# The last stage of a decoder block's kernel joined to its trunk's program part

## What is computed

```python
h = rmsnorm(x, g_pre) * (1 + scale) + shift
p = h @ w_in                                   # 1024 -> 8704, cut into branches
# four token mixers: pooling, gated recurrence, short convolution, differential attention
gates = sigmoid(m_g)                           # 4 x 1024 columns of p
merged = (gates[0] * (y_pool @ w_merge_pool) + gates[1] * (y_hgrn @ w_merge_hgrn)
        + gates[2] * (y_conv @ w_merge_conv) + gates[3] * (y_diff @ w_merge_diff))
out = merged @ w_out
x = x + gate * rmsnorm(out, g_post)
```

## Time and profile before

| | us |
|---|---|
| median of 3 runs | 2377.98 (2377.79 to 2378.16) |
| profiled execution | 2383.72 |
| its span, first to last instruction | 2381.9 |
| TensorE busy in it | 2238.5 |
| VectorE, ScalarE, GpSimd busy | 1500.5, 1137.0, 849.5 |
| mean granted clock of TensorE | 0.973 |

### The profile page before, as it was taken

One profiled execution on the slowest core, in us unless ns is written; L12 is line 12 of the kernel. 1 busy time (PEld: TensorE's weight loads), 2 busy tenths in 40 slices (PEclk: granted clock), 3 DMA queues, 4 the chain that ended last, 5 costly groups with the idle time before them and its releaser, 6 DMA issues. The chain is left out here.

```text
span 2381.9 us, 35169 instructions
## 1 busy us (share of the span) xinstructions
PE 2238.5 (94%) x11573; PEld 1858.6 (78%) x11573; DVE 1500.5 (63%) x2681; ACT 1137.0 (48%) x2416; POOL 849.5 (36%) x747
## 2 busy tenths in 40 slices
PE   4798999999999999899999999999999978899998
PEld 4587788877777778787888888878888856787886
DVE  6766777748888795445777666445556436375571
ACT  4653566635454444444666666333434234444351
POOL 1222333426565563021232222133434206254452
PEclk7899999999999999999999999999999989999999
DMA  7778888678777778947566565588878766465561
GB/s 268 275 232 305 271 261 265 230 256 291 267 248 263 254 241 277 338 140 236 169 183 182 156 194 157 166 277 244 251 239 255 220 255 236 158 222 194 185 225 62
DMA packets 336940, 544.82 MB, mean 229 GB/s; under 512 B 26592, under 2 KB 216448, under 8 KB 331904
## 3 DMA queue, kind: packets, MB, share of 16 engines
q1 hardware_dynamic: 306528, 432.56, 54.4%
q10 hardware_dynamic: 30240, 110.11, 14.8%
HBM read 326.04 MB, written 221.77 MB: 230 GB/s over the span
## 5 line engine op out<-in xcount | busy, mean ns | idle before, releaser
L1791 PE MATMUL gb<-h_hi,w_both 128*128 128x512 f32 x1904 | 782.5, 411 | 54.2 <-ACT o L1013 25.5
L1793 PE MATMUL gb<-h_hi,w_both 128*128 128x512 f32 x1904 | 753.4, 396 | 0.0
L1792 PE MATMUL gb<-h_lo,w_both 128*128 128x512 f32 x1904 | 751.4, 395 | 0.0
L1791 PEld LDWEIGHTS gb<-h_hi,w_both 128*128 128x128 f32 x1904 | 363.7, 191 | 136.1 <-issue 64.4
L1793 PEld LDWEIGHTS gb<-h_hi,w_both 128*128 128x128 f32 x1904 | 362.6, 190 | 80.1
L1792 PEld LDWEIGHTS gb<-h_lo,w_both 128*128 128x128 f32 x1904 | 364.7, 192 | 66.8 <-issue 0.2
L1013 ACT ACTIVATE o<-gb 128x512 f32<-128x512 f32 x272 | 161.6, 594 | 343.1 <-PE gb L1793 297.6
L1078 ACT ACTIVATE C_prob<-C_sc,C_negm 128x512 f32<-128x512 f32 (+3 forms) x320 | 198.4, 622 | 223.4 <-DVE C_negm L1411 214.5
L881 POOL TENSOR_TENSOR C_prob<-C_prob,C_cf 128x512 f32<-128x512 f32 (+3 forms) x160 | 160.6, 1028 | 367.9 <-DVE C_cf L1433 363.3
L1323 DVE TENSOR_TENSOR o<-gb,o 128x512 f32<-128x512 f32 x204 | 140.1, 687 | 200.8 <-PE gb L1793 191.5
L1313 DVE TENSOR_TENSOR w_both<-w,w_both 128x512 fp32r<-128x512 f32 x190 | 164.9, 868 | 128.7 <-ACT w_both L990 128.3
(11 more groups left out here) (236 smaller groups left out, 3757.9 us busy)
## 6 DMA issues: line engine op xcount, KB each, us to landing
wS_scratch<-w_both SPq DMA_DIRECT2D x210, 512.0 KB, 3.7
w_both<-wS_scratch ACTq DMA_DIRECT2D x210, 512.0 KB, 4.6
w<-in_w_in_dram SPq DMA_DIRECT2D x76, 512.0 KB, 5.2
gT_scratch<-o SPq DMA_DIRECT2D x128, 256.0 KB, 4.9
D_gate<-gT_scratch SPq DMA_DIRECT2D x32, 1024.0 KB, 5.0
pT_scratch<-o SPq DMA_DIRECT2D x80, 256.0 KB, 4.4
D_wm_stage<-wm_scratch SPq DMA_DIRECT2D x32, 640.0 KB, 6.1
C_qt<-qB_scratch SPq DMA_DIRECT2D x128, 128.0 KB, 3.6
```

The costliest lines, as they stand in the source:

```text
L1791: mm(to, hi[:, k, :], h_hi[j][:, k, :], start=(fresh and k == 0), stop=False, skip_group_check=True)
L1792: mm(to, hi[:, k, :], h_lo[j][:, k, :], start=False, stop=False, skip_group_check=True)
L1793: last = mm(to, lo[:, k, :], h_hi[j][:, k, :], start=False, stop=(k == KH - 1), skip_group_check=True)
```

## The change

The last stage is now a class `LastStage`, whose parts for each engine are called at the end of the trunk's lists. The second block, with the leaving of the first, is gone. Its semaphores are those of the trunk's beginning, used again. Its text in the loops is the same but for these points:

- **Loads beside the last products.** SP issues y of the first group in slot 468 (behind `mixers_over(1)`), merge weights 0 in slot 470, gates 0 and 1 in 472 and 473, merge weights 1 in 475, each when the product whose buffers it overwrites is done. The buffers of the last stage are laid over the trunk's operands so that this is early.
- **Splits beside the last products.** Two chunks of y in each of the slots 472 to 476, weights 0 in slot 475, on ScalarE and VectorE; the first sigmoid in slot 485 of ScalarE's list.
- **Mixers.** The last eight blocks are 11 or 12 slots apart, the last at slot 452.
- **Buffers.** `wo_stage` is gone: `wo_in` has three buffers (o_buf0, o_buf1, x_in), which with post first hold y. SP issues w_out's first three slices, post, gates 2 and weights 2 only in its own part, behind the landing of all trunk outputs. The result of the squares, which nobody reads, goes into gate buffer 2 in place of wo_stage.
- **Store.** The store of a group's last block stands in step 0 ahead of the loads, in place of step 1.
- GpSimd begins when the last product is done and all outputs have landed.

```diff
-MIX_BASE = [130 + 12 * i for i in range(8)] + [372 + 25 * i // 2 for i in range(8)]
+MIX_BASE = [130 + 12 * i for i in range(8)] + [372 + 23 * i // 2 for i in range(8)]
+LAST = MIX_BASE[-1] + 16
+LAST_UNIT = PRODUCTS - PER
...
-        wo_in = (wo_stage, o_buf[0], o_buf[1], x_in)
+        wo_in = (o_buf[0], o_buf[1], x_in)
+        y_first = [y[:, :] for y in y_stage] + [t[:, TG * z:TG * z + TG] for t in (o_buf[0], o_buf[1], x_in, post) for z in range(2)]
+        junk = gate[2][:, 0:2, :].rearrange("p b t -> p (b t)")
...
                 for d in range(KD):
                     n = KD * g + d
+                    if d == 0 and not first:
+                        store(TB * g - 1, TB - 1, row_before)
                     if not (last and d + 2 >= KD):
                         load_gates(n + 2, (d + 2) % KD, at if d + 2 < KD else at_next)
                         load_wm(n + 2, (d + 2) % KD)
                     if first and d + NW < KD:
                         load_wo(d + NW)
-                    if d == 1 and not first:
-                        store(TB * g - 1, TB - 1, row_before)
...
+                if n == LAST:
+                    mixers_over(1)
+                    last_stage.first_y(sp)
+                if n == LAST_UNIT + 1:
+                    sp.wait_ge(packed, 16 * 4 * KD)
+                    sp.wait_ge(product_done, LAST_UNIT + 1)
+                    last_stage.first_wm(sp, 0)
+                for d in range(2):
+                    if n == LAST_UNIT + 3 + d:
+                        sp.wait_ge(product_done, LAST_UNIT + 2 + d)
+                        last_stage.first_gates(sp, d)
+                if n == LAST_UNIT + 6:
+                    sp.wait_ge(product_done, LAST_UNIT + 4)
+                    last_stage.first_wm(sp, 1)
...
-            mixers_over(1)
-            sp.wait_ge(packed, 16 * 4 * KD)
-            sp.sem_clear(packed)
             for b in range(4):
                 sp.wait_ge(o_stored[b], COUNTS.o_total[UNITS - 1][b])
+            last_stage.on_sync(sp)
...
+                if 0 <= n - LAST - 4 < YC // 2:
+                    for k in range(2):
+                        last_stage.y_high(act, 0, 2 * (n - LAST - 4) + k)
+                if n == LAST_UNIT + 6:
+                    act.wait_ge(product_done, LAST_UNIT + 2)
+                    last_stage.wm_high(act, 0, 0, 0)
+                if n == SLOTS - 1:
+                    last_stage.gate_sigmoids(act, 0, 0, 0)
...
+                if 0 <= n - LAST - 4 < YC // 2:
+                    for k in range(2):
+                        last_stage.y_low(dve, 0, 2 * (n - LAST - 4) + k)
+                if n == LAST_UNIT + 6:
+                    last_stage.wm_low(dve, 0, 0)
```

More of the change, by code:

```diff
@@ L180, in banks @@
             return lambda name, shape: stack.enter_context(nc.psum_tensor(tag + name, shape, F32))
+        mem = Memory()
+        with ExitStack() as low_part:
+            sb = tensors(low_part, "D_")
+            wm = [[sb(f"wm{j}_{name}", [P, YC, P], dt) for name, dt in (("stage", F32), ("hi", F32R), ("lo", F32R))] for j in range(1)]
+            sb("pad0", [P, 2 * P])
+            mem.gate = [sb(f"gate{j}", [P, 4, TG]) for j in range(2)]
+            wm += [[sb(f"wm{j}_{name}", [P, YC, P], dt) for name, dt in (("stage", F32), ("hi", F32R), ("lo", F32R))] for j in range(1, 2)]
+            sb("pad1", [P, 2 * P])
+            mem.wo_lo = [sb(f"wo_lo{j}", [P, D], F32R) for j in range(4)]
+            mem.gate += [sb(f"gate{j}", [P, 4, TG]) for j in range(2, 4)]
+            mem.m_hi, mem.m_lo = sb("m_hi", [P, KD, TG], F32R), sb("m_lo", [P, KD, TG], F32R)
+            mem.wo_hi = sb("wo_hi", [P, KD, D], F32R)
+            wo_lo_last = [sb(f"wo_lo{j}", [P, D], F32R) for j in range(5, 8)]
+            mem.wm_stage, mem.wm_hi, mem.wm_lo = ([w[y] for w in wm] for y in range(3))
+        with ExitStack() as pair:
+            mem.pb = [None, pair.enter_context(nc.psum_tensor("D_pb1", [P, D], F32))]
         sb = tensors(ctx, "")
@@ L292, in trunk @@
             b6, b7 = ps("b6", [P, 4, P]), ps("b7", [P, 4, P])
+        with ExitStack() as fourth:
+            sb, ps = tensors(fourth, "D_"), banks(fourth, "D_")
+            mem.y_stage = [sb(f"y_stage{j}", [P, TG]) for j in range(2)]
+            mem.o_buf = [sb(f"o_buf{j}", [P, D]) for j in range(2)]
+            mem.x_in, mem.post = sb("x_in", [P, D]), sb("post", [P, D])
+            mem.y_hi, mem.y_lo = sb("y_hi", [P, YC, TG], F32R), sb("y_lo", [P, YC, TG], F32R)
+            mem.wo_lo += [sb("wo_lo4", [P, D], F32R)] + wo_lo_last
+            mem.ss, mem.rstd = sb("ss", [P, 1]), sb("rstd", [P, 1])
+            mem.mb = [ps(f"mb{b}", [P, TG]) for b in range(4)]
+            mem.pb[0] = ps("pb0", [P, D])
         w1_loaded, w2_loaded = sem("w1_loaded"), [sem(f"w2_loaded{j}") for j in range(2)]
@@ L371, in lo_count @@
             return h_lo_ready, hi_count(half, j, kk)
-        packed = x_in[0]
+        packed = start[0]
+        late = iter(start[1:])
+        last_stage = LastStage(nc, mem, lambda: next(late), x, wmP, w_out, gT, yT, post_d, out, epsb)
         block = ctx.enter_context(nc.Block())
@@ L965, in _ @@
                     decays_second(i)
+            pool.wait_ge(product_done, PRODUCTS)
+            for b in range(4):
+                pool.wait_ge(o_stored[b], COUNTS.o_total[UNITS - 1][b])
+            last_stage.on_gpsimd(pool)
         @block.scalar
```

586 lines of the change are left out of this document (282 added, 304 removed).

## The result

| | before | after |
|---|---|---|
| median, us | 2378.07 (2377.79 to 2381.64) | 2404.41 (2399.5 to 2408.93) |
| profiled execution, its span | 2383.72, 2381.9 | 2399.5, 2397.6 |

The changed kernel is slower: ratio 1.010, 95% interval 1.0088 to 1.0113, some 24 us. Forecast was 2360.6, 17 us the other way. (A fourth run of the kernel before stands in this median, so it is 0.09 above the one shown earlier.)

What follows compares the result with a forecast made beforehand. TensorE was taken to bound the trunk, with losses in the first group behind it. First group -22.2, later groups +4.8 and trunk 0 sum to -17.4, giving a median of 2360.6 us; own range 2356 to 2366, wider range 2354 to 2369.

Steps and rivals of the forecast that it cites:

- three signs of being wrong: Trunk's end moves from 1930 by over 1 us; later pitch stays 99.95 or passes 104; first-group merges take 7 us a step.
- Trunk: 0 forecast: Trunk with mixer blocks 11.5 slots apart for 12.5: no cost, as TensorE is the bound and its work is unchanged.
- Rival F: Mixers: SP's blocked loads hold output stores, so ScalarE's copy, then TensorE, waits; slower if it takes 22 us; chance 0.04.
- rival D: Last trunk products: early loads slow the trunk's own weight loads, one to three us, total 2364; chance 0.08.
- Junction: Between trunk and first merge: the wait falls to 0.9 us from 14.1, with the clock staying at the upper level.
- Rival G: Junction: y comes late as SP waits at slot 468 for the mixers' last store; 2368 at the far end; chance 0.05.
- First group: -22.2 forecast: First group of the last stage: ends at 2051.4 for 2073.6, bounds -20.5 and -24 us.
- W(d + 2) = W(d) + 19.9: First-group merges: W(d), the end of step d's split D_wm_lo, comes 19.9 us after that of two steps earlier.
- W(3): First group: end of the split D_wm_lo for merge step 3, forecast at 1956.0.
- Later groups: +4.8 forecast: Three later groups: the store ahead of gates 2 and weights 2 delays step 2 by 1.6 us in each.
- the choice between 1.53 (kept) and 2.81 (lost): Later groups, step 2: a wait of 1.6 us was taken as nearest to the 1.53 that kept the clock.
- Rival C: Later groups: the clock falls in each of three new waits, 3 x 1.6 = 4.8 us on top, 2365.4; chance 0.10.

Runs made afterwards that it cites:

- b_pitch23: Kernel before with only the last eight mixer blocks set 11 or 12 slots apart: 2391.32 us, ratio 1.0051.
- b_p23_no_root: b_pitch23 with Ln and Exp of the last eight blocks' root made plain copies, without table loads (result not the layer's): 2383.68 us, ratio 1.0017.
- a_pitch24: Changed kernel with last mixer blocks 12 slots apart, y from slot 472, last-block store in step 1, 96-byte pad: 2388.72 us, ratio 1.0038.
- a_pitch25: Changed kernel with the old mixer pitch, y from slot 475, last-block store in step 1, 96-byte pad: 2375.31 us, ratio 0.9987.
- a_p25_y_first: a_pitch25 with a 224-byte pad, gates 0 and 1 and weights 1 issued behind y when the last product is done: 2372.77 us, ratio 0.9973.
- a_align64: Changed kernel with a 32-byte pad ahead of its last region, so y_hi and y_lo begin at multiples of 64 bytes: 2396.61 us, ratio 1.0079.

## Why the prediction was wrong

- **The signs named.** Two of the three signs of being wrong came: the trunk's end moved from 1930 to 1946, and the later pitch passed 104.
- **Trunk: 0 forecast, 22 measured.** The step that failed is "TensorE's work is the same and it is the bound there; VectorE at 53% goes to 58%". A mean over 100 us said nothing of single slots. The closer pitch costs 12 us (b_pitch23), of which ScalarE's root with its two table loads makes most (b_p23_no_root: 8 of the 12). Rival F had the right side and the right place of the wait (ScalarE's copy) and asked for 22 us, but named SP's queue; between 1560 and 1900 it was ScalarE's own queue. Offsets of two blocks written under each other, 13 - 23 against -10, point at this one, but the same table missed in a_pitch24.
- **Early loads: rival D, 1 to 3 us forecast, 7.8 measured.** D priced the trunk's own weight loads, and they came late as it said. It left out the output stores behind y, on SP's own queue: four o buffers, a copy that waits 10.74 us for a landing. That is the chain which F had named for the mixers, and it stood here. The DMA engines were at 0.82 in the 10 us ahead of this, then full for 20 us while y, weights and gates (5.4 MB) came. The Trainium skill, DMA: Bandwidth & Descriptors, section Issuing engines are not separate DMA queues, speaks of transfers from SP and ACT that interleave on the same engines; rows of both queues agree (w_both on ACT's, the stores on SP's, both late at a share of 1.01).
- **Junction: right in kind.** Nothing was idle ahead of the first merge. Rival G (y comes late) did not come true: the first two chunks of y landed 4.6 and 7.0 us after their issue at 1915.28 and 1915.68, and ScalarE split them only at 1933.33, since the copy that waited for the store stood ahead of them. In the runs with the old pitch y is what TensorE waits for (9.26 in a_pitch25, 4.22 in a_p25_y_first).
- **First group: -22.2 forecast, -17.9 measured.** The chain W(d + 2) = W(d) + 19.9 held to 0.05 us: 1964.90, 1984.76 and 1974.83, 1994.70, 2014.55. Waits were forecast near 4 at 2, 4 and 6, the measured ones are 3.65 and 2.66 at 2 and 4, and 2.68, 2.69 at 5 and 7, as the odd chain began late: step 3 stands 28.7 us behind step 0, forecast 25.9, and stays 2.7 to 2.9 behind the forecast through step 7. That is the term that was mis-sized, W(3). GpSimd's first add began 9.8 us after the first merge, not 7.5 (VectorE's first product had waited for the first sigmoid until 1951.28), and the split D_wm_lo took 3.63 us, not some 2; GpSimd's 6.1 and SP's 7.7 between them were right. The last merge step took 8.6 for 6.8, behind a wait of 2.69 with 0.67 granted, and the output product 48.5 for 47.8; the missing wait of 0.9 at the junction gave that much back. The wait for D_m_lo, 1.85 for 2.3, was right. (In the working 30.5 - 27.2 is 3.3, not 2.9; the 29 us taken from it hold, 29.9 were measured.)
- **Later groups: +4.8 forecast, +17.7 measured.** Mechanism and place were right: the store at 2183.51, ScalarE 8.1 us later (7.7 forecast), a wait at step 2 ended by D_wm_lo. Its size was 2.2 for 1.6. Then the clock: the choice between 1.53 (kept) and 2.81 (lost) went to the wrong side, and waits of 2.35, 1.83 and 2.52 all lost it. The step behind that choice, that the length of the wait tells, does not hold either: in the first group of the same trace a wait of 2.66 (1984.76) kept the clock at 1.00 over the next 5 us and one of 2.68 (1994.70) brought it to 0.50. Rival C had the fall at 0.10 and its price, 1.6 each, was right. The Trainium skill, TensorE: Matmul & The Clock Gate, section HAM oscillation — how this bites in real kernels, which the prediction named for C, tells of waits of some 3 to 5 us for a DMA. The waits here were shorter, so it was no forecast of them; three of them lost the clock all the same. The rest, 2.1 a group, was in no rival: nothing in the forecast asked where the operands would lie, though the change lays every buffer anew.
- **Total.** The range ended at 2369 and slower had a chance of 0.04. The closer pitch (12 us) had been put at nothing, the early loads (8) at nothing or 1 to 3, and the later groups were 13 above their term.

What is left open: the 3.6 us of VectorE's waits at the closer pitch; why a pitch of 12 slots (a_pitch24) cost nearly as much as 11.5; what decides between clock kept and clock lost behind a wait; what chose between two paces in a_align64; and why output products with one of the eight low parts of w_out out of place ran at 0.2294, where that part alone would make 0.2270.

## What to carry to other kernels

Ahead of moving work closer on a schedule, write the fixed offsets of neighbouring pieces under each other for each engine, and count function table loads with them, and then run it, since such a table found one collision here and missed another: a mean share near a half hid 6.8 us of ScalarE without a pause. Of loads that are to run early ask what stands behind them on the same queue, and who waits for a buffer of that. After every new layout of memory compare the start-to-start time of an unchanged matmul with the one before: that takes two rows, and was 2.1 us a group here.
